# Expert weights with neighbouring rows on one partition, and the activations permuted to match

## The reference, cut to what matters

```python
D_MODEL, SEQ, N_GROUPS, EXPERTS_PER_GROUP, TOP_K, D_EXPERT = 1024, 512, 4, 8, 2, 512

def hier_moe(h, router_group, router_expert, w_gate, w_up, w_down):
    xt = h.reshape(T, D)                       # the normalised rows
    g_gate, g_idx = lax.top_k(jax.nn.softmax(xt @ router_group), 1)
    e_logits = (xt @ router_expert).reshape(T, N_GROUPS, EXPERTS_PER_GROUP)
    e_val, e_idx = lax.top_k(e_logits[jnp.arange(T), g_idx[:, 0]], TOP_K)
    gate = g_gate * jax.nn.softmax(e_val, axis=-1)
    expert = g_idx * EXPERTS_PER_GROUP + e_idx
    ...
    hb = jax.nn.silu(xb @ w_gate[e]) * (xb @ w_up[e])      # (1024, 512) each
    y = hb @ w_down[e]                                     # (512, 1024)
    ...
```

## Time and profile before

| | |
|---|---|
| median of 3 runs | 1876.57 us (1872.73 to 1877.13) |
| span of the profiled execution | 1874.8 us |
| TensorE busy | 1667.4 us (89%) |
| VectorE / ScalarE / GpSimd busy | 493.3 / 369.6 / 222.3 us |
| moved by DMA | 463.21 MB, mean 247 GB/s |
| packets of DMA | 188752, of them 187680 under 8 KB |
| expert loop, layer 0 | about 325 to 850 us |
| expert loop, layer 1 | about 1308 to 1835 us |

### The profile page before, as it was taken

One profiled execution on the slowest core, in us unless ns is written; L12 is line 12 of the kernel. 1 busy time (PEld: TensorE's weight loads), 2 busy tenths in 40 slices (PEclk: granted clock), 3 DMA queues, 4 the chain that ended last, 5 costly groups with the idle time before them and its releaser, 6 DMA issues. The chain is left out here.

```text
span 1874.8 us, 20130 instructions
## 1 busy us (share of the span) xinstructions
PE 1667.4 (89%) x7420; PEld 799.9 (43%) x7420; DVE 493.3 (26%) x1046; ACT 369.6 (20%) x599; POOL 222.3 (12%) x379
## 2 busy tenths in 40 slices
PE   7999997988988898884999999987988998899882
PEld 3444544333333333332576666644333333333331
DVE  4224524111111111114244444415111111111113
ACT  2042411111111111112344445321111111111111
POOL 2000000000000000000144444400000000000000
PEclk9998998999999999997999999998999999999996
DMA  5220034999999999995111214004999999999994
GB/s 204 90 76 25 23 135 147 347 367 379 390 368 371 374 387 373 375 369 216 59 46 46 85 51 179 1 0 159 351 370 371 394 370 369 371 391 371 367 362 152
DMA packets 188752, 463.21 MB, mean 247 GB/s; under 512 B 8208, under 2 KB 8216, under 8 KB 187680
## 3 DMA queue, kind: packets, MB, share of 16 engines
q1 hardware_dynamic: 181136, 445.25, 63.4%
q10 hardware_dynamic: 2448, 8.91, 1.3%
q0 software_dynamic: 5120, 8.40, 1.2%
HBM read 452.03 MB, written 18.89 MB: 251 GB/s over the span
## 5 line engine op out<-in xcount | busy, mean ns | idle before, releaser
L585 PE MATMUL ps<-sb_xh,sb_scr 128*64 128x512 f32 x1024 | 266.7, 667 | 37.6 <-DVE sb_scr L1486 37.6
L608 PE MATMUL ps<-sb_ring_b,sb_scr 128*64 128x512 f32 x1024 | 226.3, 592 | 0.0
L608 PE MATMUL ps<-sb_ring_a,sb_scr 128*64 128x512 f32 x1024 | 226.0, 592 | 0.0
L1523 DVE COPY sb_scr<-ps 64x512 f32<-64x512 f32 x64 | 44.4, 693 | 508.4 <-ACT sb_scr L925 508.4
L1081 POOL DMA_INDIRECT expert_rows<-sb_scr,sb_si x64 | 57.9, 905 | 1013.6 <-DVE sb_scr L1523 1013.6
L742 PE MATMUL ps<-sb_xT,sb_ring_a 128*128 128x512 f32 x384 | 170.5, 598 | 1.1 <-DVE sb_xT L1229 1.1
L585 PEld LDWEIGHTS ps<-sb_xh,sb_scr 128*64 128x64 f32 x1024 | 90.6, 151 | 167.0 <-issue 167.0
L1503 DVE TENSOR_TENSOR sb_scr<-sb_scr,ps 64x512 f32<-64x512 f32 x64 | 44.1, 690 | 395.1 <-ACT sb_scr L917 395.1
L608 PEld LDWEIGHTS ps<-sb_ring_b,sb_scr 128*64 128x64 f32 x1024 | 89.3, 137 | 129.3 <-issue 129.3
L608 PEld LDWEIGHTS ps<-sb_ring_a,sb_scr 128*64 128x64 f32 x1024 | 87.3, 137 | 132.4 <-issue 132.4
L622 PE MATMUL ps<-sb_ring_a,sb_scr 128*64 128x512 f32 x512 | 118.0, 600 | 1.1 <-issue 1.1
(11 more groups left out here) (229 smaller groups left out, 1636.5 us busy)
## 6 DMA issues: line engine op xcount, KB each, us to landing
sb_ring_b<-in_w_gate_dram SPq DMA_DIRECT2D x32, 2048.0 KB, 9.6
sb_ring_b<-in_w_up_dram SPq DMA_DIRECT2D x32, 2048.0 KB, 14.3
sb_ring_b<-in_w_down_dram SPq DMA_DIRECT2D x32, 2048.0 KB, 9.9
sb_ring_a<-in_w_gate_dram SPq DMA_DIRECT2D x32, 2048.0 KB, 9.5
sb_ring_a<-in_w_up_dram SPq DMA_DIRECT2D x32, 2048.0 KB, 14.2
sb_ring_a<-in_w_down_dram SPq DMA_DIRECT2D x32, 2048.0 KB, 10.3
sb_ring_a<-in_c_w_in_dram SPq DMA_DIRECT2D x8, 2048.0 KB, 7.8
sb_ring_a<-in_ab_w_in_dram SPq DMA_DIRECT2D x5, 2048.0 KB, 10.6
```

The costliest lines, as they stand in the source:

```text
L585: mm = nc.tensor.matmul(ps[BR][64 * z:64 * z + CAP, :], me["sel"][:, j, t * CAP:(t + 1) * CAP], xh[:, t, z * 512:(z + 1) * 512], start=(t ...
L608: mm = nc.tensor.matmul(ps[BG][64 * s:64 * s + CAP, :], me["xgT"][:, j, c * CAP:(c + 1) * CAP], wblock(r, s, NC)[:, c, :], start=(c == 0), ...
L1523: v.tensor_copy(me["rows"][0:CAP, 2 + j, 512:1024], ps[BY][64:128, :]).then_inc(drained[BY], 1)
```

## The change

The rows of an expert's weights go to the partitions in blocks of neighbours: partition p gets rows 8p to 8p + 7 of gate and up, and rows 4p to 4p + 3 of down, in every case one run of 16 KB. Chunk c of a matmul then stands for rows 8p + c (4p + c). So that the products stay the same,
- norm_rows() of n = 1 and 3 writes column 8q + c of h to column c * 128 + q of xh (reads in order, writes with steps of 128 elements);
- hidden_rows() writes column 4q + c to column c * 128 + q of hrow in the same way;
- the router's weights rt and the ffn gains, now in an SBUF tile fg of their own, are brought into this order when they are loaded: 32 small DMAs on SyncE's queue in place of one, each for 16 partitions, with runs of 36 elements (rt) or single elements (fg). Their semaphore is waited for by TensorE as before, with a new count, and now by VectorE too, in turned_rows(1, 0).

```diff
--- before.py
+++ after.py
@@ -99,6 +99,7 @@
         keep = sb("keep", [P, T])
         vec = sb("vec", [P, sum(n for _, n in COLS)])
         rt = sb("rt", [P, 2, NC, NG + NE])
+        fg = sb("fg", [P, 2, NC])
         eps_t = sb("eps_t", [P, 1])
         warm = sb("warm", [P, 1])
         ss = sb("ss", [P, 5, NT])
@@ -322,6 +323,10 @@
             for key in loads:
                 loads[key] += NE // 2
 
+        def by_partition(w):
+
+            return w.rearrange("a (p c) n -> (a p) (c n)", p=P)
+
         def wblock(r, s, n):
 
             return rings[r][:, s, :].rearrange("p (c n) -> p c n", c=n)
@@ -369,7 +374,17 @@
 
             strip(0)
             strip(1)
-            sp.dma_start(rt[:].rearrange("p a b c -> p (a b c)"), router).then_inc(router_in, 16)
+            row = 2 * NC * (NG + NE)
+            width, ffn_at = cols.shape[1], 2 * NC
+            for a in range(NC):
+                part = slice(16 * a, 16 * a + 16)
+                for l in range(2):
+                    sp.dma_start(rt[part, l, :, :], bass.AP(
+                        tensor=router.tensor, offset=(l * NC + a) * (NG + NE),
+                        ap=[[NC * row, 16], [row, NC], [1, NG + NE]])).then_inc(router_in, 16)
+                    sp.dma_start(fg[part, l, :], bass.AP(
+                        tensor=cols.tensor, offset=ffn_at + l * NC + a,
+                        ap=[[NC * width, 16], [width, NC]]), allow_slow_non_contiguous=True).then_inc(router_in, 16)
             last_of = [("xa", 3), ("ga", 3), ("q", 3), ("k", 3), ("v", 3)]
             for i in range(3, 7):
                 wait_full(sp, last_of[i - 3])
@@ -380,11 +395,11 @@
             def expert_load(l, e, j, first):
 
                 r = exp_ring(j)
-                srcs = [w[l, bass.ds(e, 1)].rearrange("a (c p) n -> p (a c) n", p=P) for w in (w_gate, w_up, w_down)]
+                srcs = [by_partition(w[l, bass.ds(e, 1)]) for w in (w_gate, w_up, w_down)]
                 for s, b in enumerate((BG, BG, BY)):
                     if not first:
                         sp.wait_ge(filled[b], e + (moe_base[l][b] - 1))
-                    sp.dma_start(wblock(r, s, (NC, NC, FC)[s]), srcs[s]).then_inc(ring_in[(r, s)], 16)
+                    sp.dma_start(rings[r][:, s, :], srcs[s]).then_inc(ring_in[(r, s)], 16)
 
             def moe_loads(l):
                 if l == 0:
@@ -405,11 +420,10 @@
                 o = ov[l]
                 with sp.If(more > 0):
                     with sp.Fori(0, NE) as e:
-                        srcs = [w[l, bass.ds(e, 1)].rearrange("a (c p) n -> p (a c) n", p=P)
-                                for w in (w_gate, w_up, w_down)]
+                        srcs = [by_partition(w[l, bass.ds(e, 1)]) for w in (w_gate, w_up, w_down)]
                         sp.wait_ge(o["pe"], e * (4 * (BLOCKS - 1)) + 1)
                         for s in range(3):
-                            sp.dma_start(wblock("a", s, (NC, NC, FC)[s]), srcs[s]).then_inc(o["w"], 16)
+                            sp.dma_start(rings["a"][:, s, :], srcs[s]).then_inc(o["w"], 16)
                     sp.wait_ge(o["pe"], NE * 4 * (BLOCKS - 1) + 1)
 
             moe_loads(0)
@@ -678,7 +692,7 @@
             def moe(l):
                 n = 2 * l + 1
                 turn_rows(n, range(2))
-                pe.wait_ge(router_in, 16)
+                pe.wait_ge(router_in, 4 * NC * 16)
 
                 dst = opens(("lgT", l))
                 for t in range(NT):
@@ -1217,11 +1231,17 @@
                 if n == 3 and t == 0:
                     wait_full(dve, ("out", 1, NT - 1, 1))
                 dve.wait_ge(rstd_ready, n * NT + t + 1)
-                v.tensor_scalar(xh[:, t, :], h[:, t, :], rstd[:, n, t:t + 1], None, ALU.mult).then_inc(xh_ready, 1)
+                src, dst = h[:, t, :], xh[:, t, :]
+                if n % 2 == 1:
+                    src = src.rearrange("p (q c) -> p q c", c=NC)
+                    dst = dst.rearrange("p (c q) -> p q c", c=NC)
+                v.tensor_scalar(dst, src, rstd[:, n, t:t + 1], None, ALU.mult).then_inc(xh_ready, 1)
 
             def turned_rows(n, t):
 
-                gain = at["mix_g" if n % 2 == 0 else "ffn_g"]
+                gain = at["mix_g"] if n % 2 == 0 else fg[:].rearrange("p l c -> p (l c)")
+                if n == 1 and t == 0:
+                    dve.wait_ge(router_in, 4 * NC * 16)
                 for half in range(2):
                     job = ("xt", n, t, half)
                     c0 = (n // 2) * NC + half * 4
@@ -1471,7 +1491,7 @@
                 st.then(v.tensor_tensor(gates[:, 1, :], gates[:, 0, :], ex[:, :, NG], ALU.mult))
 
             def times_gain(l, dst):
-                g8 = at["ffn_g"][:, l * NC:(l + 1) * NC].unsqueeze(2).broadcast_to([P, NC, CAP])
+                g8 = fg[:, l, :].unsqueeze(2).broadcast_to([P, NC, CAP])
                 return v.tensor_tensor(dst.rearrange("p (c t) -> p c t", c=NC),
                                        ps[BX][:].rearrange("p (c t) -> p c t", c=NC), g8, ALU.mult)
 
@@ -1494,13 +1514,15 @@
                 dve.wait_ge(filled[BX], e + (base[BX] + 1))
                 if not (isinstance(e, int) and e < 2):
                     dve.wait_ge(filled[BG], e + (base[BG] - 1))
-                g8 = at["ffn_g"][:, l * NC:(l + 1) * NC].rearrange("p (z c) -> p c z", z=2)
+                g8 = fg[:, l, :].rearrange("p (z c) -> p c z", z=2)
                 v.tensor_tensor(me["xgT"][:, j, :].rearrange("p (z c t) -> p c z t", z=2, c=4),
                                 ps[BX][:].rearrange("p (c z t) -> p c z t", c=4, z=2),
                                 g8.unsqueeze(3).broadcast_to([P, 4, 2, CAP]), ALU.mult).then_inc(drained[BX], 1)
 
             def hidden_rows(j):
-                return v.tensor_tensor(me["hrow"][0:CAP, :], me["silu"][64:128, j, :], ps[BG][64:128, :], ALU.mult)
+                by_q = lambda a: a.rearrange("p (q c) -> p q c", c=FC)
+                return v.tensor_tensor(me["hrow"][0:CAP, :].rearrange("p (c q) -> p q c", c=FC),
+                                       by_q(me["silu"][64:128, j, :]), by_q(ps[BG][64:128, :]), ALU.mult)
 
             def dve_expert(l, e, k, j, ahead=2):
 
```

## The result

The changed kernel takes 1879.54 us (median of 18 runs, 1875.66 to 1884.62), the kernel before beside it 1874.97 us (18 runs, 1870.38 to 1879.07): a ratio of 1.0025, interval 1.0016 to 1.0035. That is 4.6 us slower: less than the 0.3% that the prediction took as the least that can be told from no change, but with 18 runs of each kernel the interval lies above 1. The forecast was 1897 us, some 20 us slower. The profiled execution is the quickest of its kernel: its span is 1873.6 us, 1.2 us under that of before. Lines have moved by some 14 to 21: L585 is now L599, L608 is L622, L614 is L628, L622 is L636, L1503 is L1524, L1220 is L1238, L1486 is L1506.

The account below looks back on a forecast made before the run. Bound: TensorE's matmul time plus a hole waiting for silu, L1503 and VectorE. Span 1874.8 + 34.1 (write) + 0.5 + 2.1 (normalised rows) - 16 (clock) = 1895.5 us, 1897 against the runs' median; range 1873 to 1930.

Parts of the forecast that it names:

- What bounds the kernel: Expert loops: period is matmul time plus a hole where TensorE waits for silu, L1503 and what follows on VectorE.
- The loads, at nothing: Expert weight loads in 16 KB rows: no TensorE wait for a transfer, so 0 us, both bounds 0.
- 11 us of cover: Up weights land near 616.3, their matmuls start at 627.47; cover is gone only if a load takes 11 us more.
- 15.3 us of DMA per period: Three 2048 KB transfers per expert need 15.3 us at 410 GB/s, against a period of 16.5 or more.
- The range of rates: Lone 2 MB transfers land after 7.8 us (16 KB rows) or 7.6 (2 KB); 3% gives 15.8 us, under the period.
- The write of L1503: VectorE's hidden_rows() product, written in 512 B steps: 0.69 becomes 1.22 us, 64 times, +34.1 us; bounds 0 and +138.
- The normalised rows: L1220 before each expert layer, writes at half rate, 0.753 to 1.28 us: +0.5 in layer 0, +2.1 in layer 1.
- The small loads: 32 router loads on SyncE's queue, 13.8 us of issues; fourth input weight still issued near 45.84; cost 0.
- The clock: TensorE's half-clock stretches behind the hole, at L585: longer period and hole take half away, -16 us.
- the strided write is free: Rival, chance 0.37: L1503 stays at 0.69 and L1220 at 0.75 us; 1877 us, at most +3.
- the clock gives nothing back: Rival, chance 0.12: the write costs its cycle, low stretches as often or oftener; +37 to +57, 1913 to 1933 us.
- the clock makes it faster: Rival, chance 0.07: write costs little, say 10 us in all, shifted period empties the low stretches; -23, 1854 us.

Follow-up runs that it names:

- p256: Kernel before plus one extra 64 x 256 VectorE product in front of hidden_rows, into rows no one reads; 1878.76 us, ratio 1.0020.
- r_before: Kernel before, reordered: half of pick_rows() in front of turn_hidden(), selection before the wait for silu; 1774.70 us, ratio 0.9465.
- e1: Changed kernel with both strided writes back in order, so only the weights' layout differs from the kernel before (experts multiply wrong rows); 1873.76 us, ratio 0.9989.
- e3: Kernel before with only gate and up weights by partition, and normalised rows, gains and router permuted; 1875.01 us, ratio 1.0002.
- p448: Kernel before plus one extra 64 x 448 VectorE product in front of hidden_rows; 1901.07 us, ratio 1.0163.
- r_after: Changed kernel, reordered: half of pick_rows() in front of turn_hidden(), selection before the wait for silu; 1760.19 us, 0.9371 of the kernel before.

## Why the prediction was off

**What bounds the kernel.** Right. The period was matmul time plus the hole; lengthening the hole by 0.34 us in p256 lengthened the period by 0.34 us, and covering it in r_before took 100.9 us away, where the two waits of the earlier trace rows are 103.4 us together. That the two numbers are so near is chance. By the profiled executions the two waits shrink by 96.2 us (4.8 and 2.4 are left), TensorE's busy time by 22.2 us, as low stretches are gone, and 16.0 us of waits in front of L609 are new: 102.4 us, where the spans differ by 101.8.

**The loads, at nothing.** Right, in e1 and e3. The argument by 11 us of cover and by 15.3 us of DMA per period held, and r_before shows its other side: where TensorE needs 15.0 us for an expert, the loads, at 15.2, are the bound. The range of rates that I had taken from two lone transfers (3%) was met by 413 against 428 GB/s (3.6%), with the sign turned: 16 KB runs are the faster ones when DMA never rests.

**The write of L1503. This is the step that failed**, in the words of the prediction: "I take the middle one, one more cycle for each element: 0.69 becomes 1.22 us. 64 x 0.53 = +34.1 us". The direction, the place and who waits were right; the size was 0.33 us and 20.7 us in all. The price came from a difference of 4 ns over four elements in L1433 and L1469, 1.0 ns for each, and was carried over to 512 elements; the runs show 0.65 ns for each over 512. The bounds, 0 and +138 us, held, so the mechanism was right and this term of the sum was sized too high. 13.4 of the 16.1 us between the forecast difference (+20.7) and the measured one (+4.6) lie here. The Trainium skill's Advanced Engine Details and Errata, SBUF Cachelines, agrees with the sign both for the 512 B write (690 to 1023 ns) and for the 16 B reads (690 to 1044 ns), and gives no size. What the Trainium skill's VectorE: DVE Perf Modes, Mode 1×, says, one result a cycle with any strides, doesn't hold here: the same 512 results took 333 and 354 ns more with such steps.

**The normalised rows.** The sum was near: +2.6 us forecast, some 2.1 measured, though the pieces differ (1.7 of it is in layer 1's transposes L474, busy 5.60 instead of 3.93 us). VectorE's timeline in layer 1:

```profile
1265.95 3.66 DVE L1238 TENSOR_SCALAR sb_xh<-sb_h,sb_rstd 128x1024 f32<-128x1024 f32 x3
```

Three that stand in line take 3.66 us, 1.22 each, where 1.28 was forecast. By itself each of the eight changed instructions takes 1.31 to 1.36 us; they overlap a little.

**The small loads.** Cost nothing, as forecast, but the issues took longer than the 13.8 us worked out for them. SyncE's timeline:

```profile
30.62 0.66 SPq L382 DMA_DIRECT2D sb_rt<-in_router_dram  x1
31.32 0.60 SPq L385 DMA_DIRECT2D sb_fg<-in_cols_dram  x1
...
52.27 0.59 SPq L351 DMA_DIRECT2D sb_ring_a<-in_ab_w_in_dram  x1
```

32 issues took 21.65 us, and the fourth input weight went out at 52.27 instead of 45.84. The prediction had said near 45.84, so this sign failed; the matmuls of that weight come some 55 us later, and TensorE does not wait for it.

**The clock.** -16 was forecast and about -18 came, for the wrong hole. With the right price of the write the sum would have been 20.7 + 2.6 - 16 = +7.3 us. For the hole that was forecast, 34.1 - 16 = +18.1 us stands against p448's +27.5 (+24.9 without the run that stands apart): 19.6 us came back in its quickest run, and by the spans some 9 and 3 us in the next two (1896.6 and 1901.9 us, where 1871.6 of the kernel before and 33.6 us of hole make 1905.2). The clock term came out near by luck more than by reasoning: the rows of before gave the spacing of the stretches, but not how it answers to a change.

**The rivals.** That the strided write is free fell (1023 against 690 ns), though its time, 1877, is as near to the result as any. That the clock gives nothing back fell with 245.5 us at L599. That the clock makes it faster was the nearest in mechanism: it needed a price under 0.25 us with half of the stretches gone, and 0.33 us with some two thirds gone came out just on the other side by the medians; by the profiled executions alone, 1.2 us faster, it would have held.

## What to carry to other kernels

- A layout that makes transfers more efficient is worth nothing while no one waits for a transfer; first compare bytes per period over the rate with the period. Here the order of two instructions came first (101 us), and the layout then gave another 14.5.
- If a permutation has to be paid somewhere, put it on an instruction that ends in somebody else's wait. The same steps cost 20.7 us in the product that TensorE waits for and nothing that could be told in TensorE's own transposes.
- Don't carry a difference of a few ns over four elements to 512; where a forecast hangs on one price, give both prices a forecast of their own.

## What the runs showed of the hardware

- VectorE, float32, 64 x 512 product from SBUF and PSUM: 690 ns in order, 1023 ns with results written 512 B apart, 1044 ns with both inputs read 16 B apart. A 128 x 1024 product with a per-row scalar: 753 ns in order, 1309 to 1362 ns with results written in steps of 512 B.
- TensorE's transposes of 64 x 128 blocks read in steps of 16 B: 286 instead of 228 ns each in the mean.
- Loads that are always queued move 413 GB/s in runs of 2 and 4 KB and 428 GB/s in runs of 16 KB. The Trainium skill's DMA: Bandwidth & Descriptors, Where 436 GB/s comes from, names 435 GB/s for the ports and some 358 for one core's share of the memory, and says that the latter binds; in these runs, on one core, it did not.
- A small load of 128 pieces costs SyncE 0.60 us to issue in the median; in the loops a 2 MB gate load in 16 KB runs costs 0.33, in 2 KB runs 0.37.
- The granted clock's low stretches (a half, 1.2 GHz, for a few us behind the hole of an expert) didn't come oftener in step with the hole: 19 of 64 experts at a hole of 1.5 us, 7 to 9 of 64 at 1.9, at 2.1 nine or fewer in one run and, by the mean clock, more in others, about four in six at 2.5. With the hole covered the granted clock was 1.00 throughout the stretches from 400 to 700 us and from 1300 to 1700 us, in r_before and in r_after.
